# Mask added on VectorE and probabilities normalised there, in a two-layer decoder trunk on one core

## The reference, cut to what matters

```python
score = einsum('bqh,bqhs->bqs', w_idx * H_IDX**-0.5, relu(rel))
_, idx = top_k(where(key_pos <= t, score, NEG), 64)       # DSA: selected keys
logits = q_lat . c_kv / 8 + bias[bucket(dist)]            # only over idx, dist >= 0
p = softmax(logits); o_a = (p @ c_kv) @ w_uv
logits = q . k / 8 + cum_q - cum_k                        # FoX, causal
p = softmax(logits); o_f = p @ v
h = h + concat(o_a, o_f) @ w_out
```

## Time and profile before

| what | us |
|---|---|
| median of 3 runs | 1002.54 (1002.11 to 1002.65) |
| profiled execution, its own time | 1002.46 |
| its span, first to last instruction | 1000.5 |
| outside the span | 1.96 |
| busy PE, VectorE, ScalarE, Pool | 989.8, 759.5, 538.6, 139.6 |

### The profile page before, as it was taken

The page is one execution under the profiler, slowest core; times in us unless marked ns, Lnnn a source line. Parts: engine busy times, 40 slices in busy tenths (PEclk is TensorE's granted clock), DMA queues, the critical chain, the costliest instruction groups (busy, mean ns, idle before and its releaser), DMA issues.

```text
span 1000.5 us, 16509 instructions
## 1 busy us (share of the span) xinstructions
PE 989.8 (99%) x5631; PEld 842.5 (84%) x5631; DVE 759.5 (76%) x1523; ACT 538.6 (54%) x977; POOL 139.6 (14%) x155
## 2 busy tenths in 40 slices
PE   9999999999999999999999999999999999999997
PEld 8888888888878888888888888889887788888885
DVE  6887777688667887777788777777886688777775
ACT  5555555565565555555555555555755555555553
POOL 3000000018761000000000000000287500000001
PEclk9999999999999999999999999999999999999999
DMA  8665556775534655555536555554563546555541
GB/s 303 209 207 188 187 183 190 248 240 177 190 110 148 227 189 189 189 189 189 189 128 213 196 186 187 189 185 137 198 213 130 172 147 224 190 189 189 189 147 42
DMA packets 38164, 184.75 MB, mean 185 GB/s; under 512 B 3904, under 2 KB 8176, under 8 KB 23920
## 3 DMA queue, kind: packets, MB, share of 16 engines
q1 hardware_dynamic: 33408, 178.60, 54.0%
q10 hardware_dynamic: 4720, 5.67, 1.8%
HBM read 183.18 MB, written 2.64 MB: 186 GB/s over the span
## 4 chain that ended last, share of the span: by engine, by line
PE 94%; DVE 3%; POOL 1%; ACT 1%; DMA 0%; issue 0%; DVEq 0%
PE ps L645 33%; PE ps L646 17%; PE ps L639 12%; PE ps L641 12%; PE ps L640 12%; PE ps L897 1%; DVE xboth L1162 1%; PE ps L909 1%; PE ps L731 1%; POOL rstd L295 1%; PE ps L888 1%; PE ps L884 1%; DMA cst<-consts 0%; PE ps L655 0%; PE ps L659 0%
## 5 line engine op out<-in xcount | busy, mean ns | idle before, releaser
L645 PE MATMUL ps<-xboth,whi 128*128 128x512 f32 x1440 | 508.5, 395 | 0.0
L646 PE MATMUL ps<-xboth,wlo 128*128 128x256 f32 x1440 | 403.7, 280 | 0.0
L645 PEld LDWEIGHTS ps<-xboth,whi 128*128 128x128 f32 x1440 | 270.0, 188 | 64.7 <-issue 1.0
L646 PEld LDWEIGHTS ps<-xboth,wlo 128*128 128x128 f32 x1440 | 272.0, 189 | 3.5
L1120 DVE TENSOR_TENSOR wlo<-raw,whi 128x1024 fp32r<-128x1024 f32 (+1 forms) x214 | 250.6, 1206 | 5.7 <-ACT whi L386 5.7
L386 ACT CAST whi<-raw 128x1024 fp32r<-128x1024 f32 (+1 forms) x222 | 217.6, 1030 | 7.4 <-PE ps L641 7.4
L1126 DVE TENSOR_TENSOR wlo<-raw,whi 128x1024 fp32r<-128x1024 f32 (+1 forms) x110 | 132.2, 1202 | 98.8 <-ACT whi L390 98.8
L426 ACT ACTIVATE sig<-hg 128x256 f32<-128x256 f32 x88 | 36.9, 419 | 198.8 <-DVE hg L1207 182.2
L390 ACT CAST whi<-raw 128x1024 fp32r<-128x1024 f32 (+1 forms) x112 | 112.8, 1007 | 52.2 <-PE ps L641 52.0
L639 PE MATMUL ps<-whi,hhi 128*128 128x512 f32 x352 | 138.7, 394 | 0.4 <-DVE hlo L1226 0.4
L641 PE MATMUL ps<-whi,hlo 128*128 128x512 f32 x352 | 138.9, 395 | 0.0
(11 more groups left out here) (184 smaller groups left out, 1194.2 us busy)
## 6 DMA issues: line engine op xcount, KB each, us to landing
raw<-stream SPq DMA_DIRECT2D x111, 1024.0 KB, 5.1
raw<-stream SPq DMA_DIRECT2D x113, 512.0 KB, 3.6
decay<-table ACTq DMA_DIRECT2D x2, 1024.0 KB, 8.2
table<-table ACTq DMA_DIRECT2D x1, 1524.0 KB
X<-x SPq DMA_DIRECT2D x2, 512.0 KB, 5.3
bias<-table ACTq DMA_DIRECT2D x1, 1024.0 KB, 5.9
raw<-stream SPq DMA_DIRECT2D x2, 256.0 KB, 6.2
fgain<-final_gain ACTq DMA_DIRECT2D x1, 512.0 KB, 6.7
```

What stands on the lines that cost most here:

```text
L645: nc.tensor.matmul(ps[:, bank, :], a[0], xboth[:, k, :], start=k == 0, stop=False)
L646: return nc.tensor.matmul(ps[:, bank, 0:S], a[1], xhi[:, k, :], start=False, stop=k == KT - 1)
```

## The change

It takes the mask matmuls off PE: VectorE computes drop x NEG + bias into `lg` ahead (`masked`), and `maxima` adds that in place of the bias. It takes `share` off Pool: VectorE takes one reciprocal for two heads and multiplies by four tensor_scalars. `front(6)`, `back(6)`, `front(7)` and `back(7)` move within VectorE's list. Pool's additions of the causal mask to the decay wait for the exp of heads 3 and 5 instead. The spread of the latent's 1/rms goes from the middle of QI+2 to the middle of QI+3, and VectorE does both halves of `front(2)` and the log gates ahead of it. In FFN1 Pool splits the back of chunk 0 instead of VectorE. At the start the eight idle matmuls between the transposes go, and so does the making of `nident`.

```diff
         def _(pool):
-            nc.gpsimd.memset(mone[:], -1.0)
...
-            def share(l, hh):
-                n, s = l * 2 * NH + hh + 1, hh % 4
-                pool.wait_ge(pr_out, n)
-                nc.gpsimd.tensor_tensor(rinv[:, :, hh], rsum[:, :, hh], mone[:, :], ALU.pow).then_inc(rinv_out, 1)
-                pool.wait_ge(rinv_out, n)
-                for b, at, m in ((0, slice(0, P), P), (1, slice(P, S3), S)):
-                    t = nc.gpsimd.tensor_tensor(pr[:, s, at], pr[:, s, at], rinv[:, b, hh:hh + 1].to_broadcast([P, m]),
-                                                ALU.mult)
-                t.then_inc(prn_out, 1)
...
                 power(l * 3)
+                pool.wait_ge(diag_out, l * 3 + 1)
+                split_back(l, 0)
...
-                for hh in range(2 * NH):
-                    share(l, hh)
-                    if hh == 1:
-                        pool.wait_ge(decay_in, (l + 1) * 16)
-                        pool.wait_ge(const_in, 16)
-                    if hh in (1, 3):
-                        nc.gpsimd.tensor_tensor(decay[:, :, (hh - 1) * P:hh * P], ...).then_inc(decay_set, 1)
+                pool.wait_ge(decay_in, (l + 1) * 16)
+                pool.wait_ge(const_in, 16)
+                for i in range(2):
+                    pool.wait_ge(pr_out, l * 2 * NH + (2 * i + 4))
+                    nc.gpsimd.tensor_tensor(decay[:, :, 2 * i * P:(2 * i + 1) * P], ...).then_inc(decay_set, 1)
...
-                    if n == 0:
-                        idle((8, 2)[b])
+                    if n == 0 and b == NB - 1:
+                        idle(2)
...
-                    for i in range(2):
-                        if g == 0:
-
-                            nc.tensor.matmul(ps[:, LOGB + i, 0:S3], nident[:], drop[:], start=True, stop=True)
...
-                                         start=g == 1, stop=True, skip_group_check=True)
+                                         start=True, stop=True)
...
-                tile(QI + 2, back(1), FRONT, latent_rows)
+                tile(QI + 2, back(1), FRONT)
...
-                tile(QI + 3, s, 0)
+                tile(QI + 3, s, 0, latent_rows)
...
-                pe.wait_ge(drop_out, l + 1)
...
-                if g == G_FFN1:
-                    split_back(l, 0)
...
+                    if (f, phase) == (0, 0):
+                        dve.wait_ge(w_back, chunk(l, 0) + 1)
...
+                def masked(h):
+
+                    if h >= 4:
+                        dve.wait_ge(pr_out, l * 2 * NH + (h - 3))
+                    for at, n in ((slice(0, P), P), (slice(P, S3), S)):
+                        t = nc.vector.scalar_tensor_tensor(out=lg[:, h % 4, at], in0=drop[:, at], scalar=NEG,
+                                                           in1=bias[:, h, S - n:S], op0=ALU.mult, op1=ALU.add)
+                    t.then_inc(masked_out, 1)
...
-                        add = bias[:, h, S - n:S] if g == 0 else decay[:, h, at]
+                        add = lg[:, s, at] if g == 0 else decay[:, h, at]
...
+                def share(p):
+
+                    hh = 2 * p
+                    dve.wait_ge(pr_out, l * 2 * NH + (hh + 2))
+                    nc.vector.reciprocal(rinv[:, :, hh:hh + 2], rsum[:, :, hh:hh + 2]).then_inc(rinv_out, 1)
+                    dve.wait_ge(rinv_out, l * NPAIR + (p + 1))
+                    for i in range(2):
+                        for b, at in ((0, slice(0, P)), (1, slice(P, S3))):
+                            t = nc.vector.tensor_scalar(pr[:, (hh + i) % 4, at], pr[:, (hh + i) % 4, at],
+                                                        rinv[:, b, hh + i:hh + i + 1], None, ALU.mult)
+                        t.then_inc(prn_out, 1)
...
-                front(2, (0,))
-                dve.wait_ge(crstd_out, l + 1)
...
+                front(2)
                 dve.wait_ge(lz_out, l + 1)
                 nc.vector.tensor_tensor(logf[:], mz[:], lz[:], ALU.subtract).then_inc(logf_out, 1)
...
-                front(2, (1,))
+                dve.wait_ge(crstd_out, l + 1)
+                for b in range(NB):
+                    t = nc.vector.tensor_scalar(diag_hi[:, b, :], ident, crstd[:, b:b + 1], None, ALU.mult)
+                t.then_inc(cdiag_hi_out, 1)
+                dve.wait_ge(cdiag_hi_out, l + 1)
+                diagonal_low(crstd).then_inc(cdiag_out, 1)
+                back(2)
                 dve.wait_ge(crows_mm, l + 1)
                 nc.vector.tensor_tensor(cn, ct, ps[:, CB, 0:S], ALU.mult).then_inc(cn_out, 1)
-                back(2)
...
-                dve.wait_ge(w_front, chunk(l, NF + 6) * 2)
-                front(6, (0,))
+                dve.wait_ge(bias_in, 16)
+                dve.wait_ge(drop_out, l + 1)
+                masked(0)
+                masked(1)
                 tile_sum(7)
-                front(6, (1,))
-                back(6)
-                dve.wait_ge(bias_in, 16)
...
                     if p == 0:
+                        dve.wait_ge(w_front, chunk(l, NF + 6) * 2)
+                        front(6, (0,))
                         tile_out(FX + 4, FILLB)
-                        front(7)
+                        front(6, (1,))
+                        share(0)
+                        masked(2)
+                        masked(3)
+                        back(6)
                         tile_out(FX + 5, FILLB)
                     if p == 1:
-                        back(7)
+                        front(7, (0,))
                         tile_out(FX + 6, FILLB)
                         turned(0)
+                        share(1)
+                        front(7, (1,))
                         tile_out(FX + 7, FILLB)
                         turned(1)
+                        masked(4)
+                        masked(5)
+                        back(7)
...
                     if 2 <= p <= NPAIR:
                         turned(2 * p - 2)
+                        if p < NPAIR:
+                            share(p)
                         if p == 4:
                             front(9, (1,))
                         if p == 6:
                             front(10, (1,))
                         turned(2 * p - 1)
+                    if p == 2:
+                        masked(6)
+                        masked(7)
...
-            nc.vector.tensor_scalar(nident[:], ident, NEG, None, ALU.mult).then_inc(nident_set, 1)
```

More of the change, by code:

```diff
@@ L115, in trunk @@
         tri = sb("tri", [P, NB, S], F32R)
-        nident = sb("nident", [P, P], BF16)
         bias = sb("bias", [P, NH, S])
@@ L156, in trunk @@
         rinv = sb("rinv", [P, NB, 2 * NH])
-        mone = sb("mone", [P, NB])
         ohi = sb("ohi", [P, KT, S], F32R)
@@ L201, in trunk @@
         table_out, bias_in, out_done = sems("table_out bias_in out_done")
-        half_set, nident_set, rb_set, tab_mm, tab_sb = sems(
-            "half_set nident_set rb_set tab_mm tab_sb")
+        half_set, rb_set, tab_mm, tab_sb = sems("half_set rb_set tab_mm tab_sb")
         hi_front, hi_back = sems("hi_front hi_back")
@@ L226, in trunk @@
         qk_mm, lg_out, pr_out = sems("qk_mm lg_out pr_out")
+        (masked_out,) = sems("masked_out")
         tr_mm, prT_out, pv_mm = sems("tr_mm prT_out pv_mm")
@@ L305, in split_front, with split_back @@
                                         ALU.subtract).then_inc(w_front, 1)
-            def split_back(l, m):
-                k = NF + m
+            def split_back(l, k):
                 s, at = k % 2, slice(FRONT, CHUNK)
-                pool.wait_ge(w_back, chunk(l, k))
+                if chunk(l, k):
+                    pool.wait_ge(w_back, chunk(l, k))
                 pool.wait_ge(hi_back, chunk(l, k) + 1)
@@ L357, in _ @@
                 scale(l, 1, 2)
-                split_back(l, 4)
+                split_back(l, NF + 4)
                 scale(l, 2, 3)
@@ L363, in _ @@
                 scale(l, 4, NWIDE)
-                for hh in range(2 * NH):
-                    share(l, hh)
-                    if hh == 1:
-                        pool.wait_ge(decay_in, (l + 1) * 16)
-                        pool.wait_ge(const_in, 16)
-                    if hh in (1, 3):
-                        nc.gpsimd.tensor_tensor(decay[:, :, (hh - 1) * P:hh * P], decay[:, :, hh // 2 * P + P:hh // 2 * P + S],
-                                                cmask[:, P:S].unsqueeze(1).to_broadcast([P, NH, P]), ALU.add
-                                                ).then_inc(decay_set, 1)
+                pool.wait_ge(decay_in, (l + 1) * 16)
+                pool.wait_ge(const_in, 16)
+                for i in range(2):
+                    pool.wait_ge(pr_out, l * 2 * NH + (2 * i + 4))
+                    nc.gpsimd.tensor_tensor(decay[:, :, 2 * i * P:(2 * i + 1) * P], decay[:, :, i * P + P:i * P + S],
+                                            cmask[:, P:S].unsqueeze(1).to_broadcast([P, NH, P]), ALU.add
+                                            ).then_inc(decay_set, 1)
```

(12 more changed lines are left out.)

## The result

The changed kernel takes 1007.36 us, the median of 6 runs (1006.66 to 1009.74), against 1002.6 for the kernel before beside it. The ratio is 1.0052, 95% interval [1.0042, 1.0062]: slower by half a per cent. The profiled execution took 1006.88 us with a span of 1005.1. The forecast was 1003.4, which it called no change, and its range ended at 1006.5: the prediction was wrong. The change costs 4.8 us where 0.9 was forecast.

The account below looks back on a forecast made before the run. PE's list was taken to set the time, with each PE wait paid in full. Gains of 5.4 us against losses of 6.3 gave net +0.9 on the profiled 1002.46: 1003.4 us, called no change, range 1000.0 to 1006.5.

Parts of the forecast that it names:

- Beside Pool: In attention, Pool's two mask additions beside VectorE's work cost 0 to 0.9 us each; 0.35 each taken, 0.7 a layer.
- the second addition would cost nothing: In attention, if only two-source operations suffered beside Pool, its second mask addition is free and the end 0.7 us lower.
- The start and FFN1: Dropping the eight idle matmuls at the start wins 0.9 us; Pool's split of chunk 0's back in FFN1 wins 0.4.
- The spread: Latent's 1/rms spread moved to QI+3: PE's wait before it goes, winning 0.75 us a layer, 1.5 in all.
- The mask matmuls: In attention, taking them off PE wins 0.33 us for each of four pairs in two layers, 2.6 us.
- The share: In attention, one pair's reciprocal and four tensor_scalars take VectorE 1.15 us.
- Pairs 4 and 6: At `attend`, share plus half a front between the `turned` copies makes PE wait 0.9 us each, 1.8 a layer.
- Pairs 3, 5 and 7: In attention, share between the two `turned` copies is hidden from PE, with 0.3 us to spare.
- Pair 2 apart from Pool: In attention, masked, back(7) and share make PE wait 0.35 and another 0.3 us, 0.65 a layer.
- Rival C: In attention, share is the new bound at 1.55 us a pair, losing 4.6 us a layer: 1006.3 us; chance 0.23.
- the 3 to 10: Sign for attention: the prediction is wrong if PE's waits there sum to under 3 or over 10 us.

Follow-up runs that it names:

- the second experiment: The changed kernel with Pool's second mask addition waiting for the maxima of head 6 instead of the exp of head 5: 1003.11 us, ratio 1.0007.
- the fifth: The changed kernel with both Pool mask additions behind the maxima of head 6 and the half fronts of chunks 9 and 10 behind the second `turned` copy: 999.73 us.
- The single edits: Eight idle matmuls put back into the 999.31 us kernel: 999.46 us; the same matmuls alone taken out of the kernel before: 1002.09 us against 1002.4.
- the third experiment: The changed kernel with the half fronts of chunks 9 and 10 behind the second `turned` copy at pairs 4 and 6: 1005.87 us, ratio 1.0037.
- the two best kernels: The changed kernel with both mask additions late and half fronts behind the second `turned` copy: 999.73 us; the same with FFN1's back on VectorE again: 999.31 us.

## Why the prediction was wrong

*The step that failed is "Beside Pool".* It took 0.35 us for each of Pool's two additions, out of 0 to 0.9, from a split that took 2.13 for 1.22 beside one. The second addition cost 1.84 us a layer at `turn(3)` (the second experiment takes just that away), the first 0.57 (the fifth takes that away). That is 2.4 a layer for 0.7, 3.4 us more over both. The upper bound was wrong in kind. The row showed what was left of an addition that had begun 0.95 us earlier. An instruction that starts right behind Pool's waits for nearly all of its 2.00, so the bound was 2.0. I also looked for the victim among the large instructions, where it was the 128x8 back of chunk 8. It stands in front of `turned(2)` in both kernels; the change made Pool's second addition start in the very moment before it.

The Trainium skill ("SBUF — State Buffer", the section "SBUF: two separate sides") calls the port pair that VectorE and Pool share an exclusive lock, held for the whole instruction, which a VectorE operation in a 2-port mode needs, and one with two SBUF inputs if Pool's instruction reads SBUF. The traces agree: 1.98, 0.62 and 0.16 us for one and the same instruction, and the copies out of PSUM not held. The products, with one SBUF input, were held to 1.85; that they ran in a 2-port mode no trace says. The prediction had cited "GPSIMD Engine Reference", which says contention and gives no size. Its sentence that the second addition would cost nothing if only two-source operations suffered was wrong on its own terms: it was a two-source split that was hit.

*The start and FFN1* were to win 1.3 us and lost 0.2 in this trace. For the start I took the distance from the second transposes to the low weights as won in full. The single edits give 0.1 to 0.3 us: the weights and the chain to the hidden rows come nearly when they did. For FFN1 I showed that Pool's split is ready in time, and didn't ask what it keeps VectorE from: `ur`, 1.67 us for 0.42. The same oversight as above, at a place where I hadn't named Pool as a neighbour at all. The size shown is small: 0.42 us between the medians of the two best kernels, which ran in different groups.

*What held.* The spread: 1.5 forecast, 1.3 measured in this trace, 1.2 alone. The mask matmuls: 2.6 forecast, 2.6 measured. The share: 1.15 forecast, 1.12 measured; by the formula of the Trainium skill ("VectorE: DVE Perf Modes", the TRN2 errata) it would have been 0.71, and the measurement decides against that. Pairs 4 and 6: 0.9 each forecast, 0.74 to 0.85 measured, and the third experiment shows that the half front between the copies is the cause. Pairs 3, 5 and 7 hide their share. Pair 2 apart from Pool: 0.65 forecast, about 0.3 left in the second experiment, of which `masked`, cheaper by 0.28, explains the greater part.

*The sum,* from 1003.4: Pool +3.4, start and FFN1 +1.5, pairs 2, 4 and 6 -1.2, the spread +0.2, the small steps -0.2, which is 1007.1; the profiled execution had 1006.9 and the median 1007.4. Rival C had given 1006.3 for a reason that didn't happen. The span of waits in attention, 7.8 us, lay inside the 3 to 10 that I had set as the mark of being right: a mark on a total could not tell one large wait from many small ones.

## What to carry to other kernels

Where Pool and VectorE both work on SBUF, lay their timelines over each other before moving either: a split with two SBUF inputs, or a product such as those of `share`, cost up to the whole length of the neighbour's instruction here, however small it was itself, and what counts is who is queued behind it. Start Pool's long instructions where VectorE reads PSUM or is idle, by a wait on a signal of VectorE itself; cutting them up shortens the longest wait and passes much of it on. When a row shows a stretched instruction, subtract the end of the neighbour from its end before using the stretch as a price.

## What the runs showed of the hardware

A wait of PE can cost more than its length. In the kernel with the normalising on Pool a wait of 2.17 us was followed by 3.2 us at the granted clock of 0.50 (1.2 GHz), 1.6 us more. In the profiled execution of the kernel after, a wait of 1.78 us was followed by none, with the clock at 1.00; but its other executions, which carry only a mean clock, had 1006.66 and 1006.75 us at 0.999, 1007.84 and 1007.9 at 0.997, and 1009.74 at 0.995. The third experiment, which keeps these waits, went from 1004.37 at 0.998 to 1007.54 at 0.994; the second, without them, stayed within 0.5 us. This fits a wait of 1.8 us that costs the clock in some executions and not in others, and it would explain why the second experiment gained 4.2 us where the waits summed to 3.6. But a mean clock of 0.997 alone proves nothing: an execution of the second experiment had it too, at 1003.06 us. No trace of a longer execution was taken, so that stays open.

A reciprocal of 128x4 ran its usual 0.17 us in the middle of Pool's additions (the row at 272.75), where the products right behind it were held: not every SBUF instruction of VectorE is kept out.

Pool is held by VectorE too. Its split at 511.34 started 0.16 us behind one of VectorE's and took 3.32 us; an equal one at 234.78 in the same trace, with no split of VectorE beside it, took 2.42.
